# A decoder block with expert retrieval: the last two token tiles over all experts in place of gathers

## The reference, cut to what matters

```
q = (hc @ w_query).reshape(128, 8, 2, 128)                  # 8 tiles of 128 tokens, 8 heads
s = einsum('thpd,pkd->thpk', q, sub_keys)
s1, i1 = top_k(s[:, :, 0], 16);  s2, i2 = top_k(s[:, :, 1], 16)
top_s, top_c = top_k(all 256 sums s1 + s2, 16)              # per token and head
idx = i1[top_c // 16] * 128 + i2[top_c % 16]                # one of 16384 experts
g = softmax(top_s)
a = gelu(einsum('thkd,td->thk', expert_down[idx], hc))      # 128 experts of 1024 per token
out = einsum('thk,thkd->td', g * a, expert_up[idx])
```

## Time and profile before

| | |
|---|---|
| median of 3 runs | 3044.11 us (3043.58 to 3044.11) |
| profiled execution, span from first to last instruction | 3041.3 us |
| busy: PE, DVE, ACT, POOL | 76%, 73%, 67%, 42% |
| moved by DMA | 1152 MB, of which 1076 MB by the gathers |

### The profile page before, as it was taken

The page is one execution under the profiler, slowest core; times in us unless marked ns, Lnnn a source line. Parts: engine busy times, 40 slices in busy tenths (PEclk is TensorE's granted clock), DMA queues, the critical chain, the costliest instruction groups (busy, mean ns, idle before and its releaser), DMA issues.

```text
span 3041.3 us, 38261 instructions
## 1 busy us (share of the span) xinstructions
PE 2310.2 (76%) x13098; PEld 1887.2 (62%) x13098; DVE 2213.0 (73%) x5241; ACT 2033.8 (67%) x3757; POOL 1290.5 (42%) x1164
## 2 busy tenths in 40 slices
PE   8999889888878966777666676677777777666766
PEld 4765577776765656666656566566566666555655
DVE  7897678899965967777776666677776666777744
ACT  4234268898866756776676767766776677666665
POOL 1003144444434644454454444444444444454543
PEclk9999999999989977776677777777677777776766
DMA  6252499999999999999999999999999999999997
GB/s 232 32 209 79 163 382 417 405 401 418 413 415 403 398 419 421 420 421 421 419 419 420 417 415 415 421 415 422 420 408 419 419 417 411 419 417 421 419 421 329
DMA packets 174835, 1152.07 MB, mean 379 GB/s; under 512 B 23472, under 2 KB 25392, under 8 KB 43440
## 3 DMA queue, kind: packets, MB, share of 16 engines
q0 software_dynamic: 147984, 1075.90, 85.7%
q1 hardware_dynamic: 26656, 73.72, 6.6%
HBM read 1142.60 MB, written 5.77 MB: 378 GB/s over the span
## 4 chain that ended last, share of the span: by engine, by line
DMA 37%; DVE 21%; PE 16%; ACT 11%; issue 5%; POOL 1%; POOLq 0%; DVEq 0%; ACTq 0%
DMA pair<-in_experts_dram,idx_g 36%; DVE pair L1942 10%; PE acc_a L1563 5%; ACT pair L1719 5%; PE acc_b L1563 3%; PE pef L1538 2%; ACT w L1717 1%; ACT L1715 1%; PE acc_b L1486 1%; PE turns L1502 1%; POOL pair L1392 1%; ACT L1710 1%; ACT ga L1715 1%; DVE top_i L1870 1%; DVE staged L1871 1%
## 5 line engine op out<-in xcount | busy, mean ns | idle before, releaser
L1392 POOL DMA_INDIRECT pair<-in_experts_dram,idx_g x1024 | 1226.5, 1198 | 1431.3 <-PE acc_a L1563 803.1
L1942 DVE SCALAR_TENSOR_TENSOR pair<-pair,h 128x1024 f32<-128x1024 f32 x1024 | 1247.6, 1221 | 647.3 <-DMA pair<-in_experts_dram,idx_g 645.4
L1719 ACT ACTIVATE pair<-pair,w 128x1024 f32<-128x1024 f32 x1024 | 1176.4, 1149 | 33.3
L1563 PE MATMUL acc_a<-ident,pair 128*128 128x128 f32 x5120 | 853.1, 327 | 364.4 <-ACT pair L1719 361.0
L1563 PEld LDWEIGHTS acc_a<-ident,pair 128*128 128x128 f32 x5120 | 720.4, 170 | 488.7 <-ACT pair L1719 462.3
L1563 PE MATMUL acc_b<-ident,pair 128*128 128x128 f32 x3072 | 595.4, 362 | 288.2 <-ACT pair L1719 287.9
L1563 PEld LDWEIGHTS acc_b<-ident,pair 128*128 128x128 f32 x3072 | 489.9, 188 | 387.2 <-ACT pair L1719 381.6
L1715 ACT ACTIVATE ga<-a 128x1 f32<-128x1 f32 x1024 | 204.4, 200 | 652.5 <-DVE pair L1942 644.2
L1717 ACT ACTIVATE w<-ga,g 128x1 f32<-128x1 f32 x1024 | 301.7, 295 | 33.2
L1538 PE MATMUL pef<-h2t,wq 128*128 128x128 f32 x1536 | 198.7, 293 | 5.9 <-DMA wq<-in_w_query_t_dram 5.9
L1538 PEld LDWEIGHTS pef<-h2t,wq 128*128 128x128 f32 x1536 | 196.8, 211 | 6.2 <-issue 6.2
(11 more groups left out here) (378 smaller groups left out, 2273.3 us busy)
## 6 DMA issues: line engine op xcount, KB each, us to landing
pair<-in_experts_dram,idx_g POOLq DMA_INDIRECT x1024, 13.8
wrow<-in_w_ada_t_dram SPq DMA_DIRECT2D x12, 1024.0 KB, 6.0
pieces<-in_w_query_t_dram SPq DMA_DIRECT2D x18, 512.0 KB, 8.5
wada<-in_w_ada_t_dram SPq DMA_DIRECT2D x16, 512.0 KB, 9.7
wq<-in_w_query_t_dram SPq DMA_DIRECT2D x4, 2048.0 KB, 29.7
out_dram<-h SPq DMA_DIRECT2D x8, 512.0 KB, 8.3
wout_b<-in_w_out_dram SPq DMA_DIRECT2D x1, 4096.0 KB, 33.8
x<-in_x_dram SPq DMA_DIRECT2D x7, 512.0 KB, 12.9
```

The costliest lines, as they stand in the source:

```text
L1392: p.indirect_dma_start(pair[n % R], None, A["experts"], bass.IndirectOffsetOnAxis(ap=idx[:, t % (2 * PH), k:k + 1], axis=0)).then_inc(pair ...
L1563: last = t.matmul(accs[ACC[i]][:, k * P:(k + 1) * P], pair[n % R][:, D + k * P:D + (k + 1) * P], S.ident[:], is_transpose=True, start=n % ...
L1719: s_.activation(pair[n % R][:, D:], pair[n % R][:, D:], ACT.Copy, scale=w[:, n % NA:n % NA + 1]).then_inc(scaled, 1)
L1942: v.scalar_tensor_tensor(down, down, 1.0, h2[:, n // P, :], ALU.mult, ALU.mult, accum_out=a[:, n % NA:n % NA + 1]).then_inc(dotted, 1)
```

## The change

- **Slots.** Only tiles 0 to 5 are gathered: 768 slots in place of 1024. The searches of tiles 6 and 7 (tasks 48 to 63) are still made, and they are moved forward: `DENSE_FOUND` puts one in every 16 slots from slot 266 to 511, beside the one that tiles 2 to 5 have there. Their result is not a list of rows to gather but `lists`: for each token 128 pairs of keys and 128 gates.
- **Tiles 4 and 5** (slots 512 to 767) are summed by DVE: `add_row` multiplies the up half by w and adds it to a row accumulator in SBUF, two slots behind the `dot`. ACT's scaling and PE's `add_up` are gone from these slots. Buffers are picked by `BUF`, and POOL waits for `summed`.
- **Gate matrices** (slots 524 to 555, groups m = 0 to 63 of four tokens, two groups in a slot): DVE makes two one-hot tiles of 128x512 (`make_hot`), ACT scales one by the gates in four operations (`masks_scaled`), PE multiplies them (four products, `masks`), ACT copies the 128x512 result into `w_half` (`masks_out`). SP stores four halves of 4 MB to DRAM (`w_kept`). Four of the eight `pair` buffers lie under `w_half` and are not used from slot 524 to 556.
- **The dense part** (from slot 557): 128 chunks of 128 experts. SP loads for each chunk `down_c` and `up_c` (512 KB each, four buffers each, rows of 4 KB), and for every four chunks `w_c` (512 KB, runs of 1 KB). PE makes `first_product(c)` (8 products of 128x256), ACT its gelu (`dense_gelu`), DVE multiplies by the gates (`mask_product`, 128x256), PE makes `second_product(c)` (4 products of 128x512) two chunks behind. DVE and ACT do their part of chunk c in the slot that `CHUNK_AT` gives, one chunk in every 1.65 slots from 557 to 766. `dense_close` ends tiles 6 and 7.
- **Staging.** The last queries, of tasks up to 47, are asked by slot 518 (`LATER_AT`) and staged in SBUF; their searches go on up to slot 727. Tiles are turned again for each pair of tasks (15 turns where there were 6 for tiles 2 to 7).
- **Semaphores** of the first phase are freed before `phase_d` opens.

The core of the diff:

```diff
-    SLOTS = NT * P
+    OLD = 6
+    SLOTS = OLD * P
+    ON_PE = 4 * P
+    DT = NT - OLD
+    DENSE_TASK = OLD * PH
+    CHUNKS = PK
...
+    w_half = [place(nc, f"w_half{n}", [P, PK, HALF_T], kb) for n, kb in enumerate((32, 80))]
...
+    down_c = [place(nc, f"down_c{n}", [P, KD, PK], 32 + 4 * n) for n in range(4)]
+    up_c = [place(nc, f"up_c{n}", [P, D], 48 + 4 * n) for n in range(4)]
+    w_c = [place(nc, f"w_c{n}", [P, 2 * DT, 4, HALF_T], 64 + 4 * n) for n in range(2)]
+    zc = [place(nc, f"zc{n}", [P, DT * P], 72 + n) for n in range(8)]
...
+    LATER = [(24, 25), (32, 33), (26, 27), (40, 41), (28, 29), (34, 35), (30, 31), (42, 43), (36, 37), (44, 45), (38, 39), (46, 47)]
...
+    LATE_ASKS = sorted([(254 + 16 * j, 18 + j) for j in range(6)] + [(259 + 16 * j if j < 6 else 258 + 16 * j, dense_task(j)) for j in range(16)]
...
+    DENSE_FOUND = {dense_task(j): 266 + 16 * j for j in range(DT * PH)}
...
+    FIRST_MASK = 524
+    MASKED = {FIRST_MASK + m // 2: (m - m % 2, m - m % 2 + 1) for m in range(GROUPS_W)}
+    START = max(MASKED) + 2
+    CHUNK_AT = {}
+    for c in range(CHUNKS):
+        CHUNK_AT.setdefault(START + int(c * (SLOTS - START) / CHUNKS), []).append(c)
+    LAST_SLOT = SLOTS + 2
...
+    FOR_W = (0, 4, 5, 2)
+    for n in range(SLOTS):
+        among = [r for r in range(R) if r not in FOR_W] if FIRST_MASK <= n < START else range(R)
+        r = min(among, key=lambda k: turn_of.get(k, k - R))
+        BUF.append(r)
...
-            for i in range(1, NT):
+            for i in range(1, ON_PE // P):
...
+            def w_store(m):
+                sp.wait_ge(w_out, HALF_G * (m + 1))
+                sp.dma_start(w_kept[m].rearrange("p c t -> p (c t)"), w_half[m % 2][:].rearrange("p c t -> p (c t)")).then_inc(w_stored[m % 2], 16)
+
+            down = A["down_t"]
+            up = A["up_t"]
+            kept = w_kept.rearrange("h p (b c) t -> b p h (c t)", c=4)
+
+            def down_load(c):
+                if c >= 4:
+                    sp.wait_ge(first_done, c - 3)
+                sp.dma_start(down_c[c % 4][:].rearrange("p k n -> p (k n)"), down[c]).then_inc(down_in[c % 4], 16)
+
+            def up_load(c):
+                if c >= 4:
+                    sp.wait_ge(second_done, c - 3)
+                sp.dma_start(up_c[c % 4][:], up[c]).then_inc(up_in[c % 4], 16)
+
+            def mask_load(b):
+                if b >= 2:
+                    sp.wait_ge(z_ready, 4 * (b - 1))
+                sp.dma_start(w_c[b % 2][:].rearrange("p h c t -> p h (c t)"), kept[b]).then_inc(w_in[b % 2], 16)
+
+            for m in range(3):
+                w_store(m)
+            sp.wait_ge(w_stored[0], 32)
+            for c in range(4):
+                down_load(c)
+            for c in range(4):
+                up_load(c)
+            w_store(3)
+            sp.wait_ge(w_stored[1], 32)
+            for b in range(2):
+                mask_load(b)
+            for c in range(4, CHUNKS + 2):
+                if c < CHUNKS:
+                    if c % 4 == 0 and c >= 8:
+                        mask_load(c // 4)
+                    down_load(c)
+                if c >= 6:
+                    up_load(c - 2)
+            for i in range(ON_PE // P, OLD):
+                sp.wait_ge(fin_ready, i + 1)
+                sp.dma_start(out[i], acc_at[i][:]).then_inc(stored, 16)
...
-                if n >= R:
-                    hold(pool, up_used, n + 1 - R)
-                p.indirect_dma_start(pair[n % R], None, A["experts"],
-                                     bass.IndirectOffsetOnAxis(ap=idx[:, t % (2 * PH), k:k + 1], axis=0)).then_inc(pair_in[n % R], 16)
+                if n >= START and BUF[n] in FOR_W and BEFORE[n] < START:
+                    hold(pool, w_stored[1], 32)
+                if 0 <= BEFORE[n] < ON_PE:
+                    hold(pool, up_used, BEFORE[n] + 1)
+                elif BEFORE[n] >= ON_PE:
+                    hold(pool, summed, BEFORE[n] + 1 - ON_PE)
+                p.indirect_dma_start(pair[BUF[n]], None, A["experts"],
...
+            def masks(m):
+                if m == 0:
+                    pe.wait_ge(acc_read, ON_PE // P)
+                pe.wait_ge(hot1_ready, m + 1)
+                pe.wait_ge(hot2_scaled, 4 * (m + 1))
+                if m >= 2:
+                    pe.wait_ge(w_out, m - 1)
+                for k in range(4):
+                    last = t.matmul(pb[:, (m % 2) * 512 + k * PK:(m % 2) * 512 + (k + 1) * PK], hot1[:, m % 2, k, :], hot2[:, m % 2, k, :],
+                                    start=True, stop=True)
+                last.then_inc(w_done, 1)
+
...
+            def first_product(c):
+                pe.wait_ge(down_in[c % 4], 16 * (c // 4 + 1))
+                if c == 0:
+                    pe.wait_ge(w_out, GROUPS_W)
+                if c == 2:
+                    turns_free()
+                if c >= 4:
+                    pe.wait_ge(gelu_out, c - 3)
+                o = first_bank(c).rearrange("p (m n) -> p m n", n=P)
+                for k in range(KD):
+                    last = t.matmul(o, down_c[c % 4][:, k, :], h2[:, OLD:, k * P:(k + 1) * P], start=k == 0, stop=k == KD - 1)
+                last.then_inc(first_done, 1)
+
+            def second_product(c):
+                if c == 0:
+                    pe.wait_ge(s_out, len(GROUPS))
+                    pe.wait_ge(ya_ready, NT)
+                pe.wait_ge(z_ready, c + 1)
+                pe.wait_ge(up_in[c % 4], 16 * (c // 4 + 1))
+                for j in range(DT):
+                    for n in range(2):
+                        last = t.matmul(second_bank(j, n), zc[c % 8][:, j * P:(j + 1) * P], up_c[c % 4][:, n * 512:(n + 1) * 512],
+                                        start=c == 0, stop=c == CHUNKS - 1, skip_group_check=True)
+                last.then_inc(second_done, 1)
...
+            for c in range(CHUNKS + 2):
+                if c < CHUNKS:
+                    first_product(c)
+                if c >= 2:
+                    second_product(c - 2)
...
+            def masks_scaled(m):
+                j, q = m // (P // 4), m % (P // 4)
+                act.wait_ge(hot2_ready, m + 1)
+                for k in range(4):
...
+                s_.activation(w_half[half_ % 2][:].rearrange("p c t -> p t c")[:, first:first + 4, :],
+                              pb[:, (m % 2) * 512:(m % 2) * 512 + 512].rearrange("p (t c) -> p t c", c=PK), ACT.Copy).then_inc(w_out, 1)
...
+            def dense_gelu(c):
+                act.wait_ge(first_done, c + 1)
+                if c >= 8:
+                    act.wait_ge(second_done, c - 7)
+                s_.activation(zc[c % 8][:], first_bank(c), ACT.Gelu_apprx_tanh).then_inc(gelu_out, 1)
...
+                if n < ON_PE:
+                    act.wait_ge(w_ready, n + 1)
+                    s_.activation(pair[BUF[n]][:, D:], pair[BUF[n]][:, D:], ACT.Copy, scale=w[:, n % NA:n % NA + 1]).then_inc(scaled, 1)
...
+            def make_hot(m):
+                j, q = m // (P // 4), m % (P // 4)
+                if m == 0:
+                    dve.wait_ge(iota_made, 2)
+                    dve.wait_ge(tt_out, TT_COUNT["lists"])
+                    dve.wait_ge(q_done, len(GROUPS))
+                if m >= 2:
+                    dve.wait_ge(w_done, m - 1)
+                for to, r, ready in ((hot2, 1, hot2_ready), (hot1, 0, hot1_ready)):
+                    v.tensor_tensor(to[:, m % 2], bcast(lists_t[:, j, r, 4 * q:4 * q + 4], 2, [P, 4, PK]),
+                                    bcast(iota_row[:], 1, [P, 4, PK]), ALU.is_equal).then_inc(ready, 1)
+
+            def add_row(n):
+                i, at_ = n // P, n % P
+                dve.wait_ge(w_ready, n + 1)
+                if n > ON_PE:
+                    dve.wait_ge(summed, n - ON_PE)
+                acc, up, weight = acc_at[i][:], pair[BUF[n]][:, D:], w[:, n % NA:n % NA + 1]
+                if at_ == 0:
+                    v.tensor_scalar(acc, up, weight, None, ALU.mult).then_inc(summed, 1)
+                else:
...
+            def mask_product(c):
+                dve.wait_ge(gelu_out, c + 1)
+                if c % 4 == 0:
+                    dve.wait_ge(w_in[(c // 4) % 2], 16 * (c // 8 + 1))
+                z = zc[c % 8][:].rearrange("p (h t) -> p h t", t=HALF_T)
+                v.tensor_tensor(z, z, w_c[(c // 4) % 2][:, :, c % 4, :], ALU.mult).then_inc(z_ready, 1)
+
+            def dense_close(j):
+                dve.wait_ge(second_done, CHUNKS)
+                to = h2[:, OLD + j, :]
+                for n in range(2):
+                    half_ = slice(n * 512, (n + 1) * 512)
+                    v.tensor_tensor(to[:, half_], second_bank(j, n), gate_row[:, half_], ALU.mult).then_inc(dense_part, 1)
+                dve.wait_ge(dense_part, 2 * (j + 1))
+                v.tensor_tensor(to, to, x2_of(OLD + j), ALU.add).then_inc(fin_ready, 1)
```

More of the change, by code:

```diff
@@ L1620, in _ @@
             project_att(1)
-            for n in range(SLOTS):
+            for n in range(START):
```

(20 more changed lines are left out.)

259 lines of the change are left out of this document (207 added, 52 removed).

## The result

| | before | after |
|---|---|---|
| median (range, runs) | 3043.85 us (3041.31 to 3044.11, 4) | 2945.32 us (2938.95 to 2948.05, 4) |
| ratio, 95% interval | | 0.9678 [0.9666, 0.969] |
| profiled execution, its span | 3044.11, 3041.3 us | 2948.05, 2946.3 us |
| bytes moved | 1152 MB | 1051 MB |

A forecast was written before the change was run, and what follows sets the result against it. It took DMA traffic to bound the old kernel and PE, just longer than DMA, the new dense part. First `second_product` 1989 + 900 + waits 15 = 2904; tail 8 gives span 2912, plus 2.8 the time 2915 us; range 2862 to 3030.

The forecast's parts named there:

- Slots 0 to 520: Stretch up to tile 3's `finish`: unchanged to slot 253, then 10 us later; slot 520's dot at 1768.
- 0 to 18 us; I take 10: Slots 254 to 519: added time over 266 slots, at 2.59 against 2.52 us per slot.
- Gate stage: Slots 520 to 556: 11.5 us for the first four, then 185 us, ending at 1964.5, before the turnover's copies and store.
- I take 14 us in all: Slots 524 to 556: waits in the DVE, ACT, PE chain with two buffers, 0 to 1 us per slot.
- Turnover: At slot 557: last copies, store, then gather 557 and its first work; first `second_product` at 1989, 6 less to 15 more.
- Dense stage: From the first `second_product`: PE's remaining 873 us, 900 at clock 0.97, plus 15 of load waits, from 1989 to 2904.
- A: Dense part: PE bounds near full clock; 2915 us, own range 2875 to 2960; chance 0.55.
- B: Dense part: queue sharing makes chunk loads late, PE idles and its clock falls to 0.90; 3000 us; chance 0.22.
- C: Dense part: PE's clock drops to 0.73, making the kernel slower than before; 3211 us; chance 0.12.
- D: Dense part: DMA bounds and PE is hidden, products costing less than two records; 2881 us, 2867 without gate-stage waits; chance 0.08.
- E: Searches at two in 16 slots don't fit: 43 us in place of 39.8, 50 us in all; 2955 us; chance 0.03.
- the 240 us of bytes: Whole kernel: net 101 MB less at 420 GB/s, the gain if DMA stays the bound and never idles.

The follow-up runs named there:

- Run 11: Kernel after with Run 4's buffer change, and ACT's copy into `w_half` walking with four tokens innermost, still fp32: 2931.25 us, ratio 0.9626.
- Run 4: Kernel after, with the four buffers under the gate matrices kept out of use for slots 557 to 560 too: 2937.81 us, ratio 0.9663.
- run 2: Kernel after, with `w_c` loaded for the first eight chunks only, 15.7 MB less to read: 2914.37 us, ratio 0.9582.
- run 3: Kernel after, with the cuts of run 1 and run 2 together, less PE work and less DMA: 2888.38 us, ratio 0.9497.
- run 1: Kernel after, with a quarter of `second_product` left out, one of four products per chunk: 2940.95 us, ratio 0.9669.
- run 12: Kernel after, with Run 11's copy order and run 10's bf16 gates together, with Run 4's buffers: 2887.57 us, ratio 0.9495.
- run 10: Kernel after with Run 4's buffers and gate matrices in bf16, one `w_c` load serving eight chunks: 2942.02 us, ratio 0.9667.
- run 7: Kernel after, with four groups of gates a slot, a gate stage of 16 slots and 16 gathers moved to the dense stage: 2968.5 us, ratio 0.9754.

## Why the prediction held, and where it was off

- **Slots 0 to 520**: predicted 1769.15 for tile 3's finish, measured 1781.4. The step "0 to 18 us; I take 10" covers slots 254 to 519. Slots 254 to 511 alone cost 13.4 us, near it. What I left out is that `add_row` begins behind slot 512 and not behind slot 520: slots 512 to 519 cost 6.4 us that the sum has at nothing.
- **Gate stage**: 199.35 us predicted from finish to last store, 217.7 measured. This is the step that was most wrong. DVE's 171 us measured near 180; ACT's copy took 1.03 us where I took 0.59 from a copy of the same size that writes in order; a one-hot tile 0.68 for 0.6, a scaling 0.39 for 0.3. "I take 14 us in all" for waits was too little: PE waited 67 us for the copies. Run 11 shows the copy's part, 7 to 10 us; the rest, among it DVE's extra 9 and the two-buffer chain, was not taken apart.
- **Turnover**: 20.5 us predicted, 28.2 measured. The store took 11.1 us as forecast (11.5). The dot of gather 557 started 8.5 us behind its issue and not 5.7: I took the shortest landing, although `w_c` and three chunk loads go out with it; no run shows that they are the cause. And the first gate product stands one slot later than I put it. Run 4 removes 5.4 of it.
- **Dense stage**: 915 us predicted, 911 measured up to the last closing step. The number is right by luck, since the bound is the other one. "PE is just longer than DMA" was false, by some 30 us. PE's 873 us is right (874, run 2), and with DMA out of its way its clock is 1.00 and not 0.97, so PE needs no 900. DMA's 885 measured 897 to the end of full traffic: 410 GB/s instead of 420, so 1.05 MB take 2.56 us and not 2.49. And a stage that DMA bounds doesn't end with the traffic. PE still had 29 us to do on its buffers, a term that the sum doesn't have. 897 and 29, less the 16 us between gather 557 and the first `second_product`, are 910, close to the 915 that I had reached by 900 and 15. `w_c` at 50 us was right (run 3).
- **Tail**: 8 us predicted, 8.1 measured.
- **Rivals.** A's sum holds, its bound does not. B is a real pattern, eight waits for `down_c` up to 10 us and the lower clock behind the longer ones, but it costs PE 24 us of waits and about 11 of clock, where B had 85. C did not come near, with a mean clock of 0.99 here and 0.95 in run 1. The Trainium skill, "TensorE: Matmul & The Clock Gate", section on HAM oscillation, has a stream with DMA waits between its bursts drop to the lower clock, burst after burst. For the single wait the trace agrees: 0.50 behind the wait of 11.6 us in run 1, and behind the four named above in the kernel after. That it happens burst after burst does not hold here, because most chunks come in time: PE waits for a load eight times in 128 chunks. The lowest mean in the kernel after is the gate stage's 0.60, with PE busy 57% of the time. D named the right bound for a wrong reason, since products do cost two records. Its span of 2878 lacked 31 us up to gather 557 (2011 for 1980), 12 us of traffic and 25 at the end (38 us from full traffic to the last instruction, for 13). E: the searches fit; slots 254 to 511 cost 13.4 us, not 50.

The four misses before the tail (12, 18, 8 and -4 us) make the 34 us between the spans, 2946.3 and 2912. The "126 us less" of the prediction sets a span against a time; span against span it was 129.

Where the 240 us of bytes went: 98.5 came. The gate stage moves 242 GB/s for 215 us, 88 us of traffic not done at 410, and the turnover next to nothing for some 10 us more. From slot 254 on the mean rate is 410 and not the 418 or so of the earlier trace rows, 2% of 1600 us, 30 us. At the end PE works off its last four chunks for 29 us beside a DMA at a fifth of its rate, 23 us. These are rough and come to 151, where 141 are missing.

## What to carry to other kernels

When two resources come out within 3% of each other, leave out a part of each in turn before naming one; the sum survived here because both had nearly the same length, and the fix (fewer bytes) would have been missed by a reader who believed PE. Add to a stage bound by DMA what the engine behind it still has to do when the last load lands. Look behind the long waits before reading a mean clock. Cost a copy by its write pattern, not by its size: a walk with the near axis innermost was worth 7 us, and made bf16 gates worth 44 more (run 12 against 11), which without it were worth nothing (run 10 against 4). A stage that idles DMA while another is bound by it should keep as much traffic as it can, even if it gets longer (run 7).
